# A gated convolution layer in split float32r: the low halves of the weights come from accumulating DMAs, and some convolution taps change engines

## The reference

```python
hn = rms_norm(h, norm_g)
a, b, gate = split(hn @ w_in, 3)            # w_in: 1024 x 3072
u = a * sigmoid(b)
u = causal depthwise conv of u, 31 taps a channel, + conv_b
u = silu(layer_norm(u) * ln_g + ln_b) * silu(gate)
y = h + u @ w_out                           # w_out: 1024 x 1024
```

## Time and profile before

| | |
|---|---|
| three runs | 422.23, 424.12, 424.19 us (median 424.12) |
| profiled execution | span 422.2 us from the first to the last instruction; its own time isn't given apart from the three runs |
| mean granted clock of TensorE | 0.984 of full speed |
| busy: PE, VectorE, ScalarE, GpSimd | 390.1, 336.6, 228.2, 268.8 us |
| instructions | 4730 |
| moved by DMA | 34.06 MB, 81 GB/s on average |
| the chain that ended last, by engine | VectorE 39%, PE 26%, GpSimd 21%, issue 7%, ScalarE 4%, DMA 2% |

### The profile page before, as it was taken

How to read it: one execution, slowest core, us unless ns; L and a number is a source line. 1 busy time by engine, 2 the same in 40 slices (tenths; PEclk the granted TensorE clock), 3 DMA queues, 4 the chain that set the end, 5 groups by cost and what they waited for, 6 DMA issues and landing times.

```text
span 422.2 us, 4730 instructions
## 1 busy us (share of the span) xinstructions
PE 390.1 (92%) x1680; PEld 311.1 (74%) x1680; DVE 336.6 (80%) x392; ACT 228.2 (54%) x291; POOL 268.8 (64%) x164
## 2 busy tenths in 40 slices
PE   1689999969999599999997999999988898999996
PEld 1377888857888478888875888887866786888885
DVE  1966979899996999999999899999998947561111
ACT  5567656566556527666653757776556733550000
POOL 2469989799999938799987699999753202000000
PEclk9999999999999789999998999999998999999999
DMA  8971021111110111110111111001004161048111
GB/s 313 402 298 35 17 100 52 50 50 51 50 50 2 50 50 51 50 50 2 50 50 51 50 50 51 21 31 50 0 2 149 50 238 62 2 139 308 51 50 50
DMA packets 11831, 34.06 MB, mean 81 GB/s; under 512 B 1312, under 2 KB 1568, under 8 KB 11808
## 3 DMA queue, kind: packets, MB, share of 16 engines
q1 hardware_dynamic: 11520, 33.56, 22.4%
q10 hardware_dynamic: 288, 0.21, 0.2%
HBM read 29.57 MB, written 4.19 MB: 80 GB/s over the span
## 4 chain that ended last, share of the span: by engine, by line
DVE 39%; PE 26%; POOL 21%; issue 7%; ACT 4%; DMA 2%; SPq 0%; POOLq 0%; DVEq 0%; ACTq 0%
DVE acc L783 21%; POOL pconv L985 18%; PE acc L457 12%; PE mm L457 8%; DVE w_lo L720 5%; PE mm L421 4%; POOL x_lo L964 3%; DVE stats L800 3%; DVE dconv L759 2%; DMA sgate<-x 2%; DVE u L735 1%; ACT sgate L517 1%; DVE dconv L783 1%; PE mm L451 1%; DVE acc L772 1%
## 5 line engine op out<-in xcount | busy, mean ns | idle before, releaser
L985 POOL TENSOR_TENSOR pconv<-pconv,prod 128x512 f32<-128x512 f32 (+1 forms) x122 | 230.5, 1889 | 44.6 <-ACT prod L559 28.4
L783 DVE SCALAR_TENSOR_TENSOR acc<-u,chan,acc 128x1024 f32<-128x1024 f32 (+1 forms) x181 | 172.2, 1017 | 1.2
L421 PE MATMUL mm<-x_hi,w_hi 128*128 128x512 f32 x352 | 141.9, 403 | 10.1 <-DVEq L738 10.0
L559 ACT ACTIVATE prod<-u,chan 128x512 f32<-128x512 f32 (+1 forms) x134 | 115.1, 885 | 57.7 <-POOL pconv L985 48.8
L421 PE MATMUL mm<-x_hi,w_lo 128*128 128x512 f32 x352 | 141.1, 401 | 0.0
L421 PE MATMUL mm<-x_lo,w_hi 128*128 128x512 f32 x352 | 141.1, 401 | 0.0
L421 PEld LDWEIGHTS mm<-x_hi,w_hi 128*128 128x128 f32 x352 | 67.4, 191 | 27.6 <-issue 11.6
L421 PEld LDWEIGHTS mm<-x_hi,w_lo 128*128 128x128 f32 x352 | 67.3, 191 | 16.5
L421 PEld LDWEIGHTS mm<-x_lo,w_hi 128*128 128x128 f32 x352 | 67.3, 191 | 16.1
L720 DVE TENSOR_TENSOR w_lo<-raw,w_hi 128x1024 fp32r<-128x1024 f32 x23 | 43.7, 1898 | 8.3 <-ACT w_hi L530 8.2
L457 PE MATMUL acc<-wo_hi,x_hi 128*128 128x512 f32 x80 | 33.4, 417 | 2.9 <-DVE x_lo L835 1.7
(11 more groups left out here) (61 smaller groups left out, 384.3 us busy)
## 6 DMA issues: line engine op xcount, KB each, us to landing
raw<-w_in SPq DMA_DIRECT2D x24, 512.0 KB, 3.4
sgate<-x SPq DMA_DIRECT2D x8, 512.0 KB, 8.6
nat<-x_t SPq DMA_DIRECT2D x16, 256.0 KB, 10.7
raw<-w_out SPq DMA_DIRECT2D x8, 512.0 KB, 3.3
nat<-x SPq DMA_DIRECT2D x8, 512.0 KB, 5.5
y<-nat SPq DMA_DIRECT2D x16, 256.0 KB, 7.4
chan<-per_channel ACTq DMA_DIRECT2D x1, 140.0 KB, 4.2
ident<-identity ACTq DMA_DIRECT2D x1, 64.0 KB, 5.3
```

The costliest lines, as they stand in the source:

```text
L421: ins = nc.tensor.matmul(bank(("unit", m, h)), w[:, m % 3, k, :], xx[:, k, h * HALF:(h + 1) * HALF], start=(k == 0 and i == 0), stop=(k == ...
L559: nc.scalar.activation(prod[:, n % 3, 0:HALF * len(halves)], u_in(j, halves, k), ACT.Identity, scale=conv_w[:, j, k:k + 1], bias=conv_b[:, ...
L783: ins = nc.vector.scalar_tensor_tensor(dst, u_in(j, halves, k), w, running, ALU.mult, ALU.add)
L985: nc.gpsimd.tensor_tensor(dst, prod[:, (p - 1) % 3, width] if k == 1 else dst, prod[:, p % 3, width], ALU.add).then_inc(sums_done, 1)
```

## The change

ScalarE now writes, for every weight tile from unit 2 on and for all of w_out, a second copy, −hi, into the place of lo (an Identity with scale −1, rounded as hi is). GpSimd waits for it and issues a DMA from `raw` into that place that adds (raw − hi). VectorE's two subtractions go. PE, and SP before it reloads `raw`, wait for those DMAs' semaphores. GpSimd's program issues the DMA of unit m + 2 when it has come to the first sum planned after unit m − 1. Of w_out it issues tile 0 at tap 15 of tile 6's second half, tiles 1 to 3 at later taps, 4 and 5 after its last sum, and 6 and 7 after `inverse_deviation(1)`.

GpSimd's taps of tile 1 go from 20 to 6 and those of tile 6's second half from 26 to 20; the others are VectorE's. The join of tile 1 moves from place 20 to 12 of tile 2. The planner's unit is 11.2 us in place of 10.45, with no time off for a split, and GpSimd's room is 9.6 in place of 10.2. By this arithmetic VectorE is given 9 full steps in most units where it had 7 or 8. It comes to the end of tile 5 (162 steps of 239 now, 148 of 219 before) with unit 17 instead of 19, and to at most 220 steps before the last unit. `RSTD_TAP`, the tap of tile 6 after which GpSimd makes the first half's inverse deviation, goes from 18 to 12.

```diff
-TAPS0, TAPS1, TAPS6 = 13, 20, 26
+TAPS0, TAPS1, TAPS6 = 13, 6, 20
...
-JOINS = {0: 3, 1: 20}
+JOINS = {0: 3, 1: 12}
...
-UNIT_US, SPLIT_US, CONV_IN_US, STEP_US, SUM_US = 10.45, 1.2, 0.75, (0.67, 1.18), (1.25, 2.38)
-SUM_ROOM, FIRST_ROOM, CARRY = 10.2, 12, 1.0
+UNIT_US, SPLIT_US, CONV_IN_US, STEP_US, SUM_US = 11.2, 0.0, 0.75, (0.67, 1.18), (1.25, 2.38)
+SUM_ROOM, FIRST_ROOM, CARRY = 9.6, 12, 1.0
...
-RSTD_TAP = 18
+RSTD_TAP = 12
...
+        def wait_w_lo(engine, m):
+
+            if m < 2:
+                engine.wait_ge(wlo_ready, m + 1)
+            else:
+                engine.wait_ge(w_lo_in[m % 3], 16 * len(range(m, 1, -3)))
+
+        def wait_wo_lo(engine, r):
+
+            engine.wait_ge(wo_lo_in[r % 2], 16 * (r // 2 + 1))
...
             for m in range(2, NU):
                 kind, j = UNITS[m]
-                sp.wait_ge(wlo_ready, m - 1)
+                wait_w_lo(sp, m - 2)
...
             def project(m, h):
 
                 kind, _ = UNITS[m]
-                pe.wait_ge(wlo_ready, m + 1)
+                wait_w_lo(pe, m)
...
+                if m >= 2:
+                    nc.scalar.activation(w_lo[:, m % 3, :, :].rearrange("p k n -> p (k n)"), raw[:, m % 2, :],
+                                         ACT.Identity, scale=-1.0).then_inc(wneg_ready, 1)
...
+                nc.scalar.activation(wo[n, kp][1][:],
+                                     raw[:, m % 2, :].rearrange("p (k n) -> p k n", k=2),
+                                     ACT.Identity, scale=-1.0).then_inc(wneg_ready, 1)
...
-                if m + 2 < NU:
-                    split_w(m + 2)
-                quota = min(steps_by[m], total - 2)
+                quota = min(steps_by[m], total - STEPS_BEFORE_NORM - STEPS_AFTER_NORM - 13)
...
             moments(1)
-            for r in range(6, NWO):
-                split_wo(r)
             normalise(1)
...
+            def finish_w_lo(m):
+
+                pool.wait_ge(wneg_ready, m - 1)
+                nc.gpsimd.dma_start(w_lo[:, m % 3, :, :].rearrange("p k n -> p (k n)").bitcast(F32), raw[:, m % 2, :],
+                                    accum_op=ALU.add).then_inc(w_lo_in[m % 3], 16)
...
                 for k in taps:
+                    while due < NU and p >= (products_by[due - 3] if due > 2 else 0):
+                        finish_w_lo(due)
+                        due += 1
+                    if (j, halves, k) == (6, (1,), RSTD_TAP + 3):
+                        finish_wo_lo(0)
+                    for r, at in SPLIT_WITH.items():
+                        if p == len(PRODUCTS) - STREAM_PRODUCTS - 1 + at:
+                            finish_wo_lo(r)
...
+            for r in (4, 5):
+                finish_wo_lo(r)
             inverse_deviation(1)
+            for r in range(6, NWO):
+                finish_wo_lo(r)
```

More of the change, by code:

```diff
@@ L250, in gated_conv_layer @@
         wlo_ready = sem("wlo_ready")
+        wneg_ready = sem("wneg_ready")
+        w_lo_in = [sem(f"w_lo_in{i}") for i in range(3)]
+        wo_lo_in = [sem(f"wo_lo_in{i}") for i in range(2)]
         unit_ready = {k: sem(f"{k}_ready") for k in "abg"}
@@ L370, in _ @@
                 m = NU + r
-                sp.wait_ge(wlo_ready, m - 1)
+                if r < 2:
+                    wait_w_lo(sp, m - 2)
+                else:
+                    wait_wo_lo(sp, r - 2)
                 sp.dma_start(raw[:, m % 2, :].rearrange("p (k n) -> p k n", k=2),
@@ L480, in _ @@
                     pe.wait_ge(vlo_ready, k - AHEAD + 1)
-                    pe.wait_ge(wlo_ready, NU + (k - AHEAD) // 2 + 1)
+                    wait_wo_lo(pe, (k - AHEAD) // 2)
                     for q in range(TPH):
@@ L499, in _ @@
                     if q == TPH:
-                        pe.wait_ge(wlo_ready, NU + (KC + k) // 2 + 1)
+                        wait_wo_lo(pe, (KC + k) // 2)
                     if q == 2 * TPH:
@@ L625, in _ @@
                     copy_conv(j, h)
-                quota = min(products_by[m], PRODUCT_END[6, 0] + RSTD_TAP + 4)
+                quota = min(products_by[m], PRODUCT_END[6, 0] + RSTD_TAP + 3)
                 middle = (made + quota) // 2
@@ L636, in _ @@
                 if m == NU - 1:
-                    while made < PRODUCT_END[6, 0] + RSTD_TAP + 4:
+                    while made < PRODUCT_END[6, 0] + RSTD_TAP + 3:
                         product(made)
@@ L784, in step @@
                 ins.then_inc(steps_done, 1)
[L786 to L793, removed]
             def take_stats(g, tiles=range(NT)):
@@ L894, in _ @@
                     gate(0, 0)
-                    split_wo(0)
                     split_v(0, 0)
@@ L901, in _ @@
                     split_v(k - 1, 0)
-                if k in SPLIT_WITH.values():
-                    split_wo({n: r for r, n in SPLIT_WITH.items()}[k])
                 for _ in range(STREAM_STEPS):
@@ L965, in _, with finish_wo_lo @@
                                                 x_hi[:, k, half(h)].bitcast(F32), ALU.subtract).then_inc(xlo_pool, 1)
-            n, p = 0, 0
+            def finish_w_lo(m):
+                pool.wait_ge(wneg_ready, m - 1)
+                nc.gpsimd.dma_start(w_lo[:, m % 3, :, :].rearrange("p k n -> p (k n)").bitcast(F32), raw[:, m % 2, :],
+                                    accum_op=ALU.add).then_inc(w_lo_in[m % 3], 16)
+            def finish_wo_lo(r):
+                m = NU + r
+                pool.wait_ge(wneg_ready, m - 1)
+                nc.gpsimd.dma_start(wo[divmod(r, KC // 2)][1][:].bitcast(F32),
+                                    raw[:, m % 2, :].rearrange("p (k n) -> p k n", k=2),
+                                    accum_op=ALU.add).then_inc(wo_lo_in[r % 2], 16)
+            n, p, due = 0, 0, 2
             for j, halves, taps in GPSIMD_PARTS:
```

2 lines of the change are left out of this document (removed).

## The result

The changed kernel takes 436.66 us at the median of its 4 runs, 436.16 without the longest, against 423.22 us for the kernel before on the same chip (4 runs). The ratio, without that run, is 1.031, with a 95% interval of 1.027 to 1.034. The profiled execution took 435.0 us, its span is 433.2 (before: 422.2), so 11.0 us are to be found. The forecast was 425.0 us, its range 417 to 435: the result lies beyond both.

What follows compares the result with a forecast made beforehand. PE was taken as the bound, held up by VectorE being late. A 7.1 us gain by the projections' end shrank to 1.0 in the output; 1.9 of clock loss made net +0.9 on 424.1: 425.0 us, range 417 to 435.

Steps and rivals of the forecast that it cites:

- c: GpSimd's time to issue one accumulating DMA, taken as 1.0 us, between 0.33 and 2.5.
- d: Issue to landing of a 512 KB add, SBUF to SBUF, taken as 4.2 us, between 3.3 and 10.7.
- 2 us per issue: Rival: GpSimd pays 2 us for each DMA issue, adding 6 us: 431 us; chance 0.08.
- a slow accumulate: Rival: the read-modify-write takes 7 us, hidden in the projections, deciding at the output: 432 us; chance 0.20.
- Steps 1 to 3: Projections: PE begins unit 6 at 92.7, unit 10 at about 140, unit 16's second half at about 219.3.
- Step 3's last sentences: Projections' end: old tail of 71.4 less 0.7 us, ending at 308.0 instead of 315.1, a gain of 7.1.
- Step 4: First output weights: first product at about 311.9 against 317.7, taking 1.3 us of the gain.
- Step 5: Output tile 4: PE waits 6 us for weights 6 and 7, leaving 1.0 us gain; clock loss adds 1.9.
- The port lock: Rival: VectorE's normalisations block GpSimd's descriptor writing for weights 6 and 7, 1.5 us more: 426.5; chance 0.05.
- VectorE's relief is worth more: Rival: 30 us less VectorE work and no waits for ScalarE gain more, about 418 us; chance 0.20.

Runs made afterwards that it cites:

- e1: Changed kernel, but SyncE issues the four loads of x only once the accumulating DMAs of w_out's weights 6 and 7 have landed: 431.13 us.
- e4: Changed kernel with tile 5 transposed one unit later, so the four groups behind unit 17 become two and two: 431.39 us.
- e7: Changed kernel with all of w_out's low halves by VectorE's subtraction and tile 5 transposed a unit later: 418.04 us, 0.987 of before.
- e3: Changed kernel with the low halves of all eight w_out weights by VectorE's subtraction, DMAs kept in the projections: 422.41 us, 0.998 of before.
- e8: Changed kernel, but ScalarE copies the transposed tiles before making the next weight's high half and negated copy: 432.95 us.
- e5: Changed kernel's 30 accumulating DMAs with the taps, joins and planner rooms of the kernel before: 428.57 us, median of nine runs.
- e9: Accumulating DMAs in the projections only, w_out by VectorE, taps, joins and planner of the kernel before: 413.74 us, 0.976 of before.

## Why the prediction was wrong, by its own steps

**Prices.** c = 1.0 was near (0.88 to 0.90). d was mis-defined rather than mis-sized: the landing is counted from the issue's start, so c + d, put at 5.2, measured 4.5 in the projections. It was added up with c once too often, 0.7 us at each of two places, which doesn't matter here. The estimate from the Trainium skill (Collectives: The Full Stack, The bandwidth ceiling, with DMA: Bandwidth & Descriptors, Anatomy of one DMA) was 4.4, and the trace agrees. In the output stage the landings run from 4.6 to 9.7, with a median of 5.7. The rival "2 us per issue" falls, and so does "a slow accumulate": its 7 us were to be the price of every such DMA, and of the two that PE waits for, weight 0's takes 4.75 us (312.31 to 317.06) and weight 6's 4.9 with the loads of x away (e1). VectorE's relief by busy time is 25 us and not 30; 4.2 of the difference are the stream's gates and x_lo (14.2 and 12.0 us, 11.0 each before).

**Steps 1 to 3, up to unit 17, held in their times.** PE begins unit 6 at 92.1 (forecast 92.7), unit 10 at 139.85 (140), the second half of unit 16 at 218.79 (219.3). VectorE's last step on tile 5 ends at 236.8 (237.3), and the transposes start at 237.27. Some of it is luck. At unit 6 PE was to be ready at 90.8 and wait for VectorE; in fact VectorE frees the bank at 91.0, after a join of 1.22 us and not 2.0, and PE comes to it late, at 92.14, without a wait. The clock behind the wait at 218.79, counted at nothing, is 0.77 over 7.3 us, some 1.6 us, mostly hidden behind VectorE's tile 5.

**Step 3's last sentences failed.** "From there I take the measured tail of the projections, 71.4": the tail of before had its transposes in other places. The changed planner puts four groups behind one unit, as many as there are banks, and I subtracted 0.7 us for two of them instead of asking who frees their banks. The projections end at 313.4 and not 308.0: 3.25 us of waiting and 1.8 of clock. e4 prices this at 4.8 us, e7 against e3 at 4.4. ScalarE's negated copy ("there I cost it at nothing; without that cover it would be 1 us a unit") lost its cover exactly here: it stands before the bank copies, and e8 shows the place of w_hi and the negated copy together to be worth 3.2 us, the clock's part with it.

**Step 4** was late by 5.2 us (317.06 for 311.9) by the same loss; its own wait was 1.66.

**Step 5 named the right wait and the right chain, and missed 4.7 us of it.** From the late transposes to PE's release I had 0.7 + 2.1 + 1.3 + 5.2 = 9.3 us. In e1, without the loads of x, it is 355.99 − 346.38 = 9.6, after a wait of 6.25 where the forecast said 6. In the changed kernel it is 14.35: the landing is 9.65 us. I had taken d from idle DMA engines ("5 to 17%", which is the projections; the same rows have 39% in the stream and 25% behind it) and noted that SP's loads would wait for accumulating DMAs, but didn't follow SP's queue on to what comes next in it, the loads of x, which thereby arrived at the chain. The window there has a DMA share of 0.95. The clock's cost, put at 1.9, was 1.5 (5.3 us at 0.72). Of the prediction's own signs this one held in kind: PE's longest wait is the one in output tile 4, released by a GpSimd DMA, but it is 10.99 us and not "some 6".

**The sum.** The base was a median of 424.1 for three runs of the kernel before; with the fourth it is 423.2. In the traces that plays no part: the forecast's span is 422.2 + 0.9 = 423.1 us, the measured one 433.2, 10.1 more. Of these 5.2 are there when the stream begins, 0.4 come in the stream (29.3 us for 28.9), 5.1 from the late transposes to PE's release (14.35 for 9.3), and 0.5 go back behind it. Both large errors have one sign, and both are places where the forecast took over a stretch of the old trace though the change had moved what stands in it. Slower had the largest chance of the three, 0.39, but more than 0.3 of it came from rivals that fell; that the side came out so is luck. No case held two such losses.

**The port lock** found nothing in its favour: the issue at 351.09, with VectorE's two normalisations starting at 351.24, took 1.08 us instead of 0.86, 0.2 more and not 1.5, and the landing behind it in e1 was ordinary (4.9). The rule of the Trainium skill (SBUF — State Buffer, Who interferes with whom) may not bear on these operations; no run separates that.

**"VectorE's relief is worth more"** was right of the DMAs in the projections (e5: 8.9 us by the stream's start) and was taken back just as its "against" said, by nine steps a unit.

## What to carry to other kernels

An engine that is relieved is worth most when it is left relieved: with no tap moved the DMAs of the projections alone gain 10 us (e9), and of this gain little was left once the planner had filled VectorE up again and put four bank users behind one unit. Where a planner moves work, no stretch of the old timeline may be taken over whole, not even one without waits: list who needs which bank or buffer there, and who stands in front of the engine that frees it. And a DMA in place of a computation suits weights that are due a unit later, not one at the end of a dependency chain: its 4.5 us are latency there, and the loads that a queue held up by it issues next can fall on top. Last, where two engines meet, a small difference in order can be worth 3 us (the join in e5 and e9), so one profiled execution isn't the kernel.

## What the runs showed of the hardware

- An add of 512 KB from SBUF to SBUF takes 4.5 us from issue to landing (median of the 22 in the changed kernel's projections). Queue q0, which has these adds alone, used 19.2% of the engines' time for 15.73 MB, q1, the plain loads and stores, 22.5% for 33.56 MB: 1.8 times as much per byte. The Trainium skill (Collectives: The Full Stack, The bandwidth ceiling) has an add cost two source reads, which would double it; this trace is near that.
- Beside 2 MB of loads issued 1 to 3 us earlier the same add takes 9.65 us.
- Two waits of 1.16 and 2.09 us with 0.7 us of transposes between them (before 239.90 and 242.65) were followed by a clock of 0.95 over 35 us; with only the first of them left (e8) it was 1.00. I had not counted clock for waits of that size.
- The same wait doesn't always cost clock. Behind 2.13 us at 218.8 the clock is 0.77 over 7.3 to 7.5 us in the changed kernel, e3, e7 and e8, with part of the matmuls at the lower of the two levels (1.2 in place of 2.4 GHz, 0.63 us a matmul in place of 0.40); in e4 it is 1.00. Of e7's five runs two have a mean clock of 1.00 and take 416.40 and 416.89 us, three have 0.992 and take 418.04 to 418.41.
- VectorE's join of [128 x 1024], which reads GpSimd's `pconv`, and GpSimd's first sum of the next tile start within 0.5 us of each other, and one of them waits for the other. In e9 the join takes 1.23 us (130.94) and the sum 3.04; in e5 the join takes 4.22 (130.74) and the sum 2.70, and the join ends 1.1 us after the sum. In the changed kernel it is 1.22 once (78.44) and 3.23 once (125.09).
